# Hybrid encoder block, 1 core: gated linear attention moved out of a stage of its own into the stick-breaking stage, and the products with R on four small tiles

## The reference, cut to what matters

```
h = rmsnorm(x); proj = h @ w_in
A: stick-breaking attention, 6 heads x 64
   z = q k^T / 8 ; between = reverse cumsum of log_sigmoid(-z)
   weights = exp(log_sigmoid(z) + between), keys before the query only ; weights @ v ; head norm
B: RWKV-7, 6 heads x 64, a delta-rule state, in chunks of 64 frames
C: gated linear attention (GLA), 4 heads, dk=32, dv=64, 16 chunks of 64 frames:
   log_alpha = log_sigmoid(gd @ gate_up + gate_b) / 16
   b = cumsum(log_alpha) in the chunk
   o = (q exp(b)) @ S + tril(q k^T exp(b_t - b_s)) @ v
   S = S exp(b_last) + (k exp(b_last - b))^T v
   out = head_rmsnorm(o) * silu(g)
x = x + rmsnorm(concat(A, B, C) @ w_out)
x = x + rmsnorm(relu(rmsnorm(x) @ w_ff1)^2 @ w_ff2)
```

## Time and profile before

| | us |
|---|---|
| median of 3 runs | 1713.92 (1712.32 to 1715.52) |
| the profiled execution | 1707.59 |
| its span in the trace | 1705.7 |
| PE busy | 1526.6 (90%) |
| DVE / ACT / POOL busy | 740.4 / 537.9 / 275.3 |
| mean granted TensorE clock | 0.944 |

### The profile page before, as it was taken

How to read it: one execution, slowest core, us unless ns; L and a number is a source line. 1 busy time by engine, 2 the same in 40 slices (tenths; PEclk the granted TensorE clock), 3 DMA queues, 4 the chain that set the end, 5 groups by cost and what they waited for, 6 DMA issues and landing times. The chain is left out here.

```text
span 1705.7 us, 24803 instructions
## 1 busy us (share of the span) xinstructions
PE 1526.6 (90%) x10033; PEld 1179.7 (69%) x10033; DVE 740.4 (43%) x1164; ACT 537.9 (32%) x945; POOL 275.3 (16%) x288
## 2 busy tenths in 40 slices
PE   6889899898988367499899999999999999999997
PEld 5767688576766255245447778888888888888876
DVE  6355133747363474344544542423233333233336
ACT  4432221323222351466763331212112121212032
POOL 4435433213120100145330010000000000000000
PEclk9989999899989575699999999999999999999999
DMA  5525423314120200502025231111111020202014
GB/s 175 153 84 147 115 64 94 94 49 112 49 56 24 101 0 0 148 8 80 20 68 173 108 127 38 39 61 37 61 37 61 26 72 13 85 12 86 10 52 173
DMA packets 132975, 124.13 MB, mean 73 GB/s; under 512 B 19885, under 2 KB 111210, under 8 KB 132890
## 3 DMA queue, kind: packets, MB, share of 16 engines
q1 hardware_dynamic: 86384, 92.89, 17.6%
q10 hardware_dynamic: 46506, 30.04, 6.3%
HBM read 98.07 MB, written 24.84 MB: 72 GB/s over the span
## 5 line engine op out<-in xcount | busy, mean ns | idle before, releaser
L1782 DVE TENSOR_TENSOR bk_acc<-bk_acc,all_ps_b 128x512 f32<-128x512 f32 x128 | 88.0, 687 | 283.6 <-PE all_ps_b L1865 283.6
L1842 PE MATMUL all_ps_b<-all_hH,bk_w1L 128*128 128x512 f32 x512 | 200.2, 391 | 5.0 <-PE all_ps_b L1865 2.1
L1865 PE MATMUL all_ps_b<-bk_w2H,all_gL 128*128 128x512 f32 x512 | 199.3, 389 | 2.5 <-DVE all_gL L1772 2.5
L1842 PE MATMUL all_ps_b<-all_hH,bk_w1H 128*128 128x512 f32 x512 | 199.3, 389 | 0.0
L1842 PE MATMUL all_ps_b<-all_hL,bk_w1H 128*128 128x512 f32 x512 | 199.2, 389 | 0.0
L1865 PE MATMUL all_ps_b<-bk_w2L,all_gH 128*128 128x512 f32 x512 | 199.2, 389 | 0.0
L1865 PE MATMUL all_ps_b<-bk_w2H,all_gH 128*128 128x512 f32 x512 | 199.2, 389 | 0.0
L1092 PE MATMUL fr_ps_F<-fr_hH,fr_wL 128*128 128x512 f32 (+1 forms) x416 | 175.6, 422 | 1.8 <-DVE fr_hL L686 0.9
L1092 PE MATMUL fr_ps_F<-fr_hH,fr_wH 128*128 128x512 f32 (+1 forms) x416 | 165.9, 399 | 0.0
L1092 PE MATMUL fr_ps_F<-fr_hL,fr_wH 128*128 128x512 f32 (+1 forms) x416 | 165.7, 398 | 0.0
L1612 ACT CAST bk_w2H<-all_raw 128x1024 fp32r<-128x1024 f32 x32 | 32.9, 1047 | 355.4 <-PEq L1870 351.7
(11 more groups left out here) (338 smaller groups left out, 2445.5 us busy)
## 6 DMA issues: line engine op xcount, KB each, us to landing
fr_raw<-in_w_in ACTq DMA_DIRECT2D x37, 512.0 KB, 4.2
bk_raw<-in_w_ff SPq DMA_DIRECT2D x32, 512.0 KB, 4.5
all_raw<-in_w_ff SPq DMA_DIRECT2D x32, 512.0 KB, 4.8
projected<-fr_stage ACTq DMA_DIRECT2D x39, 256.0 KB, 4.4
fr_raw<-in_w_in SPq DMA_DIRECT2D x13, 512.0 KB, 4.2
fr_xt<-in_x SPq DMA_DIRECT2D x8, 512.0 KB, 5.1
bk_acc<-in_x SPq DMA_DIRECT2D x8, 512.0 KB, 3.4
x_after_mixers<-bk_acc SPq DMA_DIRECT2D x8, 512.0 KB, 2.6
```

Source lines behind the costliest of these rows:

```text
L1782: dve.tensor_tensor(acc[:, j, ds], acc[:, j, ds], ybank[g % 4][:], ALU.add).then_inc(collected, 1)
L1842: m = pe.matmul(bank[s][h][:], w[s][:, k, :], a[:, k, hs], start=(k == 0 and q == 0), stop=(k == KB - 1 and q == 2))
L1865: m = pe.matmul(ybank[g % 4][:], a[:, i, ts], w[:, i, ds], start=(i == 0 and q == 0), stop=(i == FB - 1 and q == 2))
```

## The change: what it does

1. `gla` is gone. `stick_breaking` becomes `heads`: the work of group C is cut into labelled pieces (`SLOTS`), for each half of the frames (512) once; piece `label` of half h is issued on its engine after unit `h * 26 + SLOTS[label]` of the 72 units. Its matrix work is now in small tiles (keys of one chunk and one head as weights, 32 rows by 64 columns). `qb` and its spreading copies are gone. Sigmoid is made as exp and log, in the table that the stage has loaded already. The states are one scan over 64 x 9 columns. The two halves are stored by four transfers.
2. PSUM: OB and X are one bank each, the other two (G) serve group C. The first half of a pair's output is taken after unit 8, the values are turned and the norm's sums made one half after the other.
3. `front`: the six products with R are issued by `crossed` on four tiles; one wait for both h, then all 24. `FILL` has other numbers. The order on DVE and ACT inside a pass changes, and `low_done`.

```diff
-    FILL = {"p1": (2,), "p2": (3,), "p3": (6,), "p4": (12,), "p5": (3,), "p6": (3,),
-            "a": (6, 2, 2, 2), "b": (4, 1, 1, 1), "c": (4, 1, 1, 1), "d": (4, 1, 1, 1),
-            "e": (8, 2, 2, 2), "f": (8, 2, 2, 2), "g1": (40, 4, 4, 4), "g2": (40, 4, 4, 4), "g3": (20, 5, 5, 5),
+    FILL = {"p1": (6,), "p2": (6,), "p3": (16,), "p4": (14,), "p5": (3,), "p6": (3,),
+            "a": (5, 2, 2, 2), "b": (4, 1, 1, 1), "c": (4, 1, 1, 1), "d": (4, 1, 1, 1),
+            "e": (6, 2, 2, 2), "f": (6, 2, 2, 2), "g1": (16, 4, 4, 6), "g2": (16, 2, 2, 6), "g3": (16, 3, 3, 6),
             "h": (3, 1, 1, 1), "z1": (2, 1, 1, 1), "z2": (2, 1, 1, 1), "z3": (2, 1, 1, 1), "z4": (2, 1, 1, 1),
-            "u": (4, 2, 2, 2), "m": (4, 2, 2, 2), "n": (3, 1, 1, 1),
-            "s0": (2, 1, 1, 1), "s1": (2, 1, 1, 1), "s2": (2, 1, 1, 1),
-            "t1": (10, 4, 4, 4), "t2": (8, 2, 2, 2), "t3": (7, 2, 2, 99)}
+            "u": (10, 2, 2, 2), "m": (10, 2, 2, 2), "n": (8, 1, 1, 1),
+            "s0": (4, 1, 1, 1), "s1": (4, 1, 1, 1), "s2": (4, 1, 1, 1),
+            "t1": (20, 3, 3, 3), "t2": (12, 2, 2, 7), "t3": (8, 2, 2, 99)}
...
             def late(k, first, then):
                 b = BT[k % 2]
+                first()
                 act.wait_ge(s("norm_kept"), k + 1)
                 act.activation(b[:], b[:], ACT.Ln).then_inc(s("ln"), 1)
                 act.wait_ge(s("ln"), k + 1)
                 act.activation(b[:], b[:], ACT.Exp, scale=-0.5).then_inc(s("rn"), 1)
-                first()
...
-                    if i + 1 == UN // 2:
-                        low_done(1)
...
                     serve(i, "t3")
+                    if i == 0:
+                        low_done(1)
...
-            low_done(0)
+                if n == 7:
+                    low_done(0)
...
+                if i:
+                    variance(i - 1)
                 invert(i)
                 serve(i, "e", "f")
                 if i:
-                    variance(i - 1)
+                    normed(i - 1)
                 if nxt:
                     early_norms(i + 1)
                     cumulate(i + 1)
-                serve(i, "g1")
-                if i:
-                    normed(i - 1)
-                if nxt:
-                    keys(i + 1)
-                    bvec(i + 1)
-                serve(i, "g2", "g3")
+                serve(i, "g1", "g2", "g3")
                 dve.wait_ge(s("back_in"), i * 16 + 16)
...
+                if nxt:
+                    keys(i + 1)
+                    bvec(i + 1)
                 serve(i, "h", "z1")
...
+                def crossed(name, left, right, needs, there):
+                    n = ORDER.index(name)
+                    for h in range(NG):
+                        grp("t_" + ORDER[n - 2], h)
+                        for need in needs:
+                            grp("t_" + need, h)
+                    for u in range(NU):
+                        for c in range(2):
+                            for h in range(NG):
+                                at, to = (c, c ^ h) if there else (c ^ h, c)
+                                m = pe.matmul(bank_of(name, h)[CH[to], chunk(u)], left(h, u)[CH[at]],
+                                              ident[CH[at], CH[at]] if right is None else right(h, u)[CH[at]],
+                                              start=True, stop=True)
+                                if u == NU - 1 and c == 1:
+                                    m.then_inc(s("m_" + name), 1)
...
+        GH, DK, DV, CH, NL, LAG = 4, 32, 64, HALF // C, 6, 26
+        SLOTS = {"gate": 0, "turn_v": 3, "diag": 6, "turn_k": 9, "kv": 11, "level0": 13, "level1": 16, "level2": 19,
+                 "out": 22, "sums": 25,
...
+                    for two in range(3):
+                        yield h, f"level{two}"
...
+                        for lv in range(2):
+                            n = 2 * two + lv
+                            d = g.D[n % 4]
+                            for c in range(CH):
+                                for hd in range(GH):
+                                    at = lv * (HALF // 2) + c * (C // 2)
+                                    mm = 1 << n
+                                    m = pe.matmul(G[hd % 2][side(hd // 2), at:at + C // 2]
+                                                  .rearrange("p (b m) -> p b m", m=mm),
+                                                  d[group(hd), chunk(c)], second(d[group(hd), chunk(c)], mm),
+                                                  start=True, stop=True)
...
-            for i in range(PAIRS):
+            load(0)
+            gla_loads(sp)
+            for i in range(1, PAIRS):
                 load(i)
+            gla_stores(sp)
             ahead.load(sp)
```

More of the change, by code:

```diff
@@ L1220, in turned, with slot @@
                         grp("t_" + ORDER[n - 2], h)
-                        grp("t_" + before, h)
-                        for u in range(NU):
-                            for c in range(2):
-                                m = pe.matmul(bank_of(name, h)[CH[c], chunk(u)], slots["R"][CH[c], h, u, :],
-                                              ident[CH[c], CH[c]], start=True, stop=True)
-                        m.then_inc(s("m_" + name), 1)
+                        for need in needs:
[9 more added lines that the diff above has]
+                                    m.then_inc(s("m_" + name), 1)
+                def slot(name):
+                    return lambda h, u: slots[name][:, h, u, :]
                 x = i % 2
@@ L2245, in stick_breaking, with __init__, sb @@
-def stick_breaking(nc, con, args, proj, ahead, banks):
+class Linear:
+    def __init__(self, nc, stack):
+        r = Region(nc, stack, "gla")
+        used = [0]
+        def sb(name, shape):
+            n = 1
+            for k in shape[1:]:
+                n *= k
+            used[0] += n
+            return r.sb(name, shape)
+        own, free = SBW // P * T, KB * T - SBW // P * T
+        CH, hole = HALF // C, free + 8 * T + 2 * D
+        r.sb("own0", [P, own])
+        self.gate = [sb(f"gate{h}", [P, 2, HALF]) for h in range(NH)]
+        self.v = [[sb(f"v{h}{n}", [P, HALF]) for n in range(2)] for h in range(NH)]
+        self.gd, self.gate_up = sb("gd", [16, T]), sb("gate_up", [16, P])
+        self.levels, self.eye = sb("levels", [P, 6, C]), sb("eye", [P, C])
+        self.x, self.e, self.cum, self.starts = [sb(n, [P, HALF]) for n in ("x", "e", "cum", "starts")]
+        self.D = [sb(f"D{n}", [P, HALF]) for n in range(4)]
+        self.A, self.vnat = sb("A", [P, 2, CH, C]), sb("vnat", [P, 2, CH, C])
+        self.knat = sb("knat", [P, CH, C])
+        self.KV, self.S, self.decay = sb("KV", [P, C, CH + 1]), sb("S", [P, C, CH + 1]), sb("decay", [P, C, CH + 1])
+        self.lg = sb("lg", [P, 2, HALF])
+        r.sb("own1", [P, hole - used[0] + own])
+        self.O, self.osq = r.sb("O", [P, 2, HALF]), r.sb("osq", [P, 2, HALF])
+        self.q, self.k = [[r.sb(f"{n}{h}", [P, HALF]) for h in range(NH)] for n in "qk"]
+        self.qin, self.kout = r.sb("qin", [P, HALF]), r.sb("kout", [P, HALF])
@@ L2250, in stick_breaking, with heads @@
+def heads(nc, con, args, proj, mixed, levels_d, ahead, banks, g):
     ident, col = con["ident"], con["col"]
@@ new lines, in issue, with advance, h_slot, chunk @@
+        def issue(pieces):
+            ahead_ = [next(pieces)]
+            def advance(unit):
+                while ahead_[0] is not None and h_slot(ahead_[0]) <= unit:
+                    ahead_[0] = next(pieces, None)
+            return advance
+        def h_slot(piece):
+            h, label = piece
+            return h * LAG + SLOTS[label]
+        def chunk(c):
+            return slice(c * C, c * C + C)
+        def group(hd):
+            return slice(DK * hd, DK * hd + DK)
+        def side(n):
+            return slice(C * n, C * n + C)
@@ L2296, in stick_breaking, with sum_bank @@
         block = st.enter_context(nc.Block())
+        def sum_bank(i, n):
+            return G[0] if i == LAST and n else X
         def span(u):
@@ L2385, in square, with log @@
                 act.activation(osq[:], O[:], ACT.Square).then_inc(s("osq"), 1)
+            def log(i, n):
+                act.wait_ge(s("o_sum"), i * 2 + n + 1)
+                act.activation(osq[:, half(n)], sum_bank(i, n)[:], ACT.Ln, scale=1.0 / DH, bias=eps[:]
+                               ).then_inc(s("o_log"), 1)
             def root(i):
[L2388 to L2390 removed]
                 act.wait_ge(s("o_log"), i * 2 + 2)
@@ L2444, in _ @@
             square(LAST)
+            for n in range(2):
+                log(LAST, n)
             root(LAST)
@@ L2590, in _ @@
                 if j == 0:
-                    squares(LAST)
+                    for n in range(2):
+                        squares(LAST, n)
 def hybrid_block(nc, args, out):
```

749 lines of the change are left out of this document (400 added, 349 removed), and 3 rows, old and new, of the table SLOTS.

## The result

The changed kernel takes 1613.1 us (median of 4 runs, 1610.3 to 1617.1) against 1714.7 for the kernel before in the same comparison: a ratio of 0.9411, 95% interval 0.9389 to 0.9434. Its profiled execution takes 1612.9, its span 1611.0. The forecast was 1577, so the gain came out as 101.6 us where 137 were expected. 1613 lies in the range that was given (1545 to 1625) and outside the forecast's own (1558 to 1597).

A forecast was written before the change was run, and what follows sets the result against it. PE was taken to bound the units, while GLA's stage was a chain with no engine near full. 1705.7 - 129.3 (GLA's stage) + 35.5 (units) - 43 (first stage) = 1568.9 in the span, 1577 us as median; range 1545 to 1625.

The forecast's parts named there:

- three signs that the prediction names for being wrong: Units taking over 230 us, the first stage ending after 545, or `back` longer than 819.
- TensorE's work in the units: GLA's small products in the units: 1472 records at 15.6 ns plus smaller terms, 31.5 us in sum.
- small tiles at two tiles' pace: Rival, units: 32-column products run at 32 ns a record, +24 us or some +17; about 1598 us; chance 0.09.
- The idle time that was to take 4 us of it: Units: some GLA pieces fall beside PE's 13.8 us of idle time, -4 us.
- I take 8 us of new PE waits: Units: PE waits from pieces added on ACT and DVE, 8 us; bounds 0 and 46.
- the interleaving stalls: Rival, units: a late GLA piece holds a softplus and so PE; 46 us in place of 8, 1615; chance 0.15.
- 13 us of steps moved into cover is the firm part: First stage: 19 projection steps moved from pass 0 ahead of the bonus product, pass 0 -13.0 us.
- They cover the 5.6 us wait: Preparation: 19 steps ahead of the bonus product cover its 5.6 us wait and 4.6 us more.
- Four tiles: First stage's six products with R: 0.75 us each instead of 1.54, up to 4.7 us shorter in a pass.
- the first stage gives little: Rival: DRAM and DVE's chain set the passes; the first stage gains only 10 us, 1610 in all; chance 0.05.
- Passes: First stage: pass 1 -12.6 us, largely from building R earlier; pass 2 -5.5; pass 3 -4.
- more than that: Rival: PE's gaps in the units swallow 10 us, no new waits, first stage -55; 1547 us; chance 0.09.

## Why the prediction was right in kind and 36 us short

Two of the three signs that the prediction names for being wrong came: the units took over 230 us (234.0), and `back` took over 819 (821.5). The first stage ended before 545, but at 537.2 and not at 516. The range held because these misses were inside its width; GLA's stage, which went whole, carries the result.

**GLA's stage** was right: all 129.3 us went, the loads in its place cost 0.2, and leaving it out of the units shows that PSUM costs nothing.

**TensorE's work in the units** was summed to 31.5 us, and 33.9 were paid. The 15.6 ns held for the levels, the largest term, on tiles that no row had shown, so the rival *small tiles at two tiles' pace* falls for them. The Trainium skill ("TensorE: Matmul & The Clock Gate", section "Wait — 56ns, not 53.3ns?") with its least distance of about 25 ns between starts does not agree with these 15.6, nor with the 17 ns of the products with A. The mis-sized term is that of the products with S, 33 ns a record for their stride: 128 x 17 ns = +2.2.

**The idle time that was to take 4 us of it** took nearly none. Without GLA's work TensorE is idle for 13.2 us, with its products alone for 12.3, and the waits are the same ones: 4.5 and 4.4 us for the softplus, 3.4 and 3.5 for q, 3.5 and 3.5 of "issue".

**"I take 8 us of new PE waits"** is the term that failed most: 19.6 us came. The loads behind it were not too low (in all 50.7 us on DVE instead of 54.8, and 33.6 on ACT instead of 36.6). DVE's pieces on 256 columns have medians of 416 to 469 ns where 420 was taken; their means of 540 to 624 come from single ones of 0.95 to 1.5 us, each beside POOL's running sum. What I did not ask is at what moment a slot comes on each engine. A softplus runs one to two units ahead of the weights of the same unit, so DVE is at slot 28 when ACT has not come to its slot 27 yet. A GLA piece whose input stands only one slot earlier on ACT holds DVE up, with the next softplus behind it. And the long waits of TensorE are followed by low clock, 5 of the 20 us, which I had not priced. Of the rival *the interleaving stalls* the mechanism is thus what happened, at under half its price (46); moving the slots took back 10 of the 20.

**The first stage, "13 us of steps moved into cover is the firm part"**: not firm. They cost nearly as much ahead of pass 0 (9.5) as they saved in it (10.3). The step that failed is "They cover the 5.6 us wait": the chain that TensorE waits for started 2.2 us later and got 7.1 us longer by the steps' work on the other engines, 2.6 of it waiting for ACT and 4.5 in DVE's instructions beside POOL's. Preparation and pass 0 together were forecast at -21 and gave -9.0; this is most of the stage's miss.

**"Four tiles", up to 12 us over the four passes** in the working (4.7, 1, 1 and 5.7), brought 2.1 (undone) to 4.1 (alone), on the edge of what can be told. TensorE's 10.4 us of saved work became 10.2 us of idle time: it waits for R and for ACT's copies, and a faster product starts the wait earlier. The rival *the first stage gives little* is right in this mechanism and too low in its total (10, not 22).

**low_done** was read rightly as 4.6 and 4.5 us of wait and is worth 10.9 alone: the largest single part that a run shows.

**Passes.** Pass 2 came out as forecast (-5.5). Pass 1 came near (-9.8, not -12.6), but that is in part luck, for the prediction gave nearly all of it to the new order on DVE. The first product with R starts 34.3 us into the pass after and 43.0 before; it starts at 36.7 with `low_done` alone in the kernel before, at 40.7 with `low_done` undone after and at 37.3 with the order undone. So most of it was the low-rank inputs' wait and some 3 us were the order. The new FILL also takes five steps (15 matmul records) out of each of passes 1 and 2, where the prediction counted one. Pass 3 had its wait for R of 5.7 us and then 16.9 us of low clock (482 to 500 us), +2.4 instead of -4; with the same first stage it takes 81.6 us in another kernel, so its sign isn't firm. `back` is 2.2 us longer, in its last stretch, where the granted clock is 0.98 and not 0.99. It is longer in all the kernels with the new units (820.0 to 821.9) than in those with the old ones (819.3 to 819.7); why, no run explains. The median lies 0.2 us above the profiled execution after, and 6.3 before, which takes 6 us off the miss. The rival *more than that* is misadded: its terms give 1551, not 1547.

## What to carry to other kernels

When work is cut into pieces beside a pipeline, compare the time at which each engine reaches a slot, not the slot's number: a piece must be late enough for the engine that runs ahead, and a long wait on the bound engine can cost about half as much again through the clock behind it. Work moved ahead of a late chain covers its wait only if none of what it asks of the other engines stands in front of the chain's instructions or slows them. A product that is made faster is worth little until the operand of the next one has been shown to be early.

## What the runs showed of the chip

- DVE and POOL hold each other up. In the first stages of five kernels (before, after and three of the runs) DVE's two-input instructions on 768 columns, the scan aside, take 0.94 to 0.96 us in all 209 cases without POOL's 128x1024 subtraction beside them. The 42 that start during one take 1.5 to 3.2 us, and each ends 0.80 to 0.83 us after it. In the 26 cases where DVE starts first, POOL takes 2.9 to 3.1 us and not 2.4.
- Tiles of 32 rows by 64, with 32 columns moving, start every 15.6 ns, just like 64x64 tiles with 64 columns: half the columns gained nothing.
- Weights read with a stride of 9 elements take 33 ns a record, side by side 17.
- ACT needs 1.09 to 1.11 us to write 512 columns with a stride (the states' decay and products), against 0.58 to 0.63 side by side.
- After waits of 4.1 and 5.7 us the granted clock is at or near its lower level in the products that follow (0.58 over 743 to 749 us, 0.50 over 482 to 498), and after one of 2.2 us (640.7) it stays at 1.00. Rows of small products twice as long contain pauses of up to 1.4 us for which the profile shows no semaphore; behind the first such row the clock is 0.57 (596 to 598).
